# Four small changes of order, of awaited counts and of the engine of a copy in a one-core decoder step

## What is computed

```python
def hybrid_layer(x, k_past, v_past, C0, n0, m0, q_start, ...):
    xn = rmsnorm(x, ln1_w)
    z = xn @ w_in                       # 1024 -> 3592 columns
    ...                                 # qa, ka, va, qm, km, vm, om, gates are columns of z
    attn = moba_attention(qa, k_all, v_all, q_start)   # softmax over own and selected blocks
    h, C, n, m = mlstm_chunkwise(qm, km, vm, i_pre, f_pre, C0, n0, m0)
    h = ... * sigmoid(om)               # norm per head, output gate
    x = x + concat([attn, h]) @ w_out
    hn = rmsnorm(x, ln2_w)
    x = x + square(relu(hn @ w_up)) @ w_down
    return x, ka, va, C, n, m
```

## Time and profile before

| | us |
|---|---|
| median of 3 runs | 699.6 |
| lowest and highest | 699.0, 699.85 |
| profiled execution | 699.11 |
| its span | 697.4 |
| PE busy | 681.3 (98%) |
| DVE busy | 449.9 (65%) |
| ACT busy | 296.3 (42%) |
| POOL busy | 322.6 (46%) |

### The profile page before, as it was taken

How to read it: one execution, slowest core, us unless ns; L and a number is a source line. 1 busy time by engine, 2 the same in 40 slices (tenths; PEclk the granted TensorE clock), 3 DMA queues, 4 the chain that set the end, 5 groups by cost and what they waited for, 6 DMA issues and landing times.

```text
span 697.4 us, 15167 instructions
## 1 busy us (share of the span) xinstructions
PE 681.3 (98%) x5547; PEld 638.8 (92%) x5547; DVE 449.9 (65%) x894; ACT 296.3 (42%) x568; POOL 322.6 (46%) x232
## 2 busy tenths in 40 slices
PE   6999999999999999999999999999999999999996
PEld 6999988788687777999999999999999999999996
DVE  4598899986243456537798685867557576585134
ACT  6532735465342233245555443343433534334222
POOL 6739999823231544247337517062260623507431
PEclk9999999999999999999999999999999999999999
DMA  7946999944486788623111323332241331413103
GB/s 246 303 122 168 281 282 277 277 136 116 143 254 204 239 283 172 168 81 122 61 59 64 121 70 127 109 118 86 87 124 69 120 108 66 130 61 121 61 1 124
DMA packets 88633, 100.41 MB, mean 144 GB/s; under 512 B 5374, under 2 KB 64338, under 8 KB 88570
## 3 DMA queue, kind: packets, MB, share of 16 engines
q1 hardware_dynamic: 74566, 92.91, 42.9%
q10 hardware_dynamic: 14004, 6.67, 4.1%
HBM read 92.92 MB, written 6.64 MB: 143 GB/s over the span
## 4 chain that ended last, share of the span: by engine, by line
PE 80%; DVE 10%; issue 3%; POOL 3%; ACT 2%; DMA 1%; DVEq 0%; POOLq 0%; ACTq 0%
PE acc L914 7%; PE acc L915 6%; PE acc L916 6%; PE acc L1417 5%; PE acc L1418 5%; PE acc L1416 5%; PE scr L1417 3%; PE scr L1418 3%; PE scr L1416 3%; PE scr L1383 3%; PE scr L1382 3%; PE scr L1384 3%; PE acc L1382 3%; PE acc L1383 3%; PE acc L1384 3%
## 5 line engine op out<-in xcount | busy, mean ns | idle before, releaser
L914 PE MATMUL acc<-act_hi,w_hi 128*128 128x256 f32 (+1 forms) x416 | 120.8, 290 | 1.1 <-DVE zT L2503 1.1
L2017 POOL TENSOR_TENSOR h_lo<-relu,h_hi 128x520 fp32r<-128x520 f32 x32 | 44.0, 1379 | 164.8 <-ACT h_hi L1803 164.5
L915 PE MATMUL acc<-act_lo,w_hi 128*128 128x256 f32 (+1 forms) x416 | 117.3, 282 | 0.0
L916 PE MATMUL acc<-act_hi,w_lo 128*128 128x256 f32 (+1 forms) x416 | 117.2, 282 | 0.0
L1502 POOL TENSOR_TENSOR w_lo<-raw,w_hi 128x1024 fp32r<-128x1024 f32 x24 | 57.2, 2387 | 97.6 <-ACT w_hi L1495 95.2
L1970 POOL TENSOR_TENSOR prod<-kv,Qb 128x1024 f32<-128x1024 f32 x32 | 85.7, 2714 | 14.1 <-DVE S L2205 11.1
L914 PEld LDWEIGHTS acc<-act_hi,w_hi 128*128 128x128 f32 x416 | 78.4, 188 | 4.0 <-issue 2.3
L915 PEld LDWEIGHTS acc<-act_lo,w_hi 128*128 128x128 f32 x416 | 78.4, 189 | 0.5
L916 PEld LDWEIGHTS acc<-act_hi,w_lo 128*128 128x128 f32 x416 | 78.3, 188 | 0.0
L2522 DVE TENSOR_TENSOR xT<-acc,xT 128x260 f32<-128x260 f32 x64 | 26.7, 426 | 48.4 <-PE acc L1418 48.4
L2503 DVE TENSOR_TENSOR zT<-acc,rstd 128x264 f32<-128x264 f32 (+1 forms) x56 | 23.5, 421 | 43.1 <-PE acc L916 40.4
(11 more groups left out here) (418 smaller groups left out, 2298.4 us busy)
## 6 DMA issues: line engine op xcount, KB each, us to landing
kv<-in_cache_k_dram SPq DMA_DIRECT2D x64, 256.0 KB, 3.4
kv<-in_cache_v_dram SPq DMA_DIRECT2D x64, 256.0 KB, 3.1
raw<-in_w_up_dram SPq DMA_DIRECT2D x16, 1024.0 KB, 5.5
raw_d<-in_w_down_dram SPq DMA_DIRECT2D x12, 1024.0 KB, 5.1
raw<-in_w_in_dram SPq DMA_DIRECT2D x14, 512.0 KB, 6.0
raw<-in_w_in_dram SPq DMA_DIRECT2D x7, 1024.0 KB, 7.4
x_tok<-in_x_prompt_dram SPq DMA_DIRECT2D x8, 512.0 KB, 5.3
raw<-in_w_out_dram SPq DMA_DIRECT2D x4, 1024.0 KB, 7.3
```

The source lines that it names most:

```text
L914: pe.matmul(out, W_HI[home(g)][:, k, :], hi[k][:, cols], start=(n == 0), stop=False)
L915: pe.matmul(out, W_HI[home(g)][:, k, :], lo[k][:, cols], start=False, stop=False)
L916: mm = pe.matmul(out, W_LO[home(g)][:, k, :], hi[k][:, cols], start=False, stop=(n == KT - 1))
L2017: pool.tensor_tensor(h_lo[:, t, :], relu2[:, t % 2, :], h_hi[:, t, :].bitcast(F32), ALU.subtract).then_inc(s_hs_lo, 1)
```

## The change

Four edits:
1. In `banks()` the first three plain products of the MLP, in accumulator banks 0, 1 and 2, wait for 70, 71 and 72 copied half groups; before, all three waited for 72. Their order is the same.
2. In `plan()` rows_M goes from slot 6 to 7, rows_s and rows_end from slot 7 to 8.
3. Of att_t (1, 0) the second piece, 128x384, is copied by ACT and no longer by DVE.
4. sm_rt and sm_r are entered ahead of sm_c, so that in slots 50 to 52 they come first. The jobs are numbered anew with them.

```diff
--- before.py
+++ after.py
@@ -159,8 +159,9 @@
     at(3, ("gates", 1), ("rstd", 0))
     at(4, ("gates", 0), ("qs_tok",))
     at(5, ("qb", 0), ("qb", 1), ("rows_f",), ("rows_sum",))
-    at(6, ("rows_max",), ("rows_M",))
-    at(7, ("rows_s",), ("rows_end",))
+    at(6, ("rows_max",))
+    at(7, ("rows_M",))
+    at(8, ("rows_s",), ("rows_end",))
     at(12, ("gcols",))
     for t in range(4):
         at(11 + 2 * t, ("tokk", t))
@@ -214,11 +215,12 @@
     at(55, ("om_mix", 2), ("om_mix", 3))
     at(46, ("sm_prep",))
     at(48, ("vs_tok",))
+    for two in range(NS // 2):
+        at(51 + two, ("sm_rt", two))
+    for two in range(NS // 2):
+        at(50 + two, ("sm_r", two))
     for b in range(NS):
         at(49 + b // 2, ("sm_c", b))
-    for two in range(NS // 2):
-        at(50 + two, ("sm_r", two))
-        at(51 + two, ("sm_rt", two))
     at(54, ("sm_den",))
     at(55, ("sm_out",), ("pv_end",))
     at(56, ("sm_rs",), ("sm_end",))
@@ -356,7 +358,7 @@
 
 def banks():
 
-    use, last = {}, {b: ("out", N_HALVES) for b in range(3)}
+    use, last = {}, {b: ("out", N_HALVES - 2 + b) for b in range(3)}
     last.update({b: ("scr", b - 4) for b in range(4, 8)})
     for kind, e in PHASES:
         if kind == "plain":
@@ -1727,7 +1729,8 @@
                     elif e == 0:
                         act.wait_ge(s_out_m, 32)
                         evacuated(act, "gcols", 0)
-                    for n, col, end_col in ((0, 0, A_COL[1]), (2, A_COL[2], PW)):
+                    parts = (0, 0, A_COL[1]), (1, A_COL[1], A_COL[2]), (2, A_COL[2], PW)
+                    for n, col, end_col in parts if (t, e) == (1, 0) else parts[::2]:
                         copy_out(pTs[e][:, col:end_col], full(act, "att_t", t, e, n)[:, 0:end_col - col],
                                  "att_t", t, e, n)
                 elif name == "mix_att":
@@ -2448,8 +2451,9 @@
                     elif e == 0:
                         dve.wait_ge(s_out_m, 32)
                         evacuated(dve, "gcols", 0)
-                    free(dve.tensor_copy(pTs[e][:, A_COL[1]:A_COL[2]],
-                                         full(dve, "att_t", t, e, 1)[:, 0:A_COL[2] - A_COL[1]]), "att_t", t, e, 1)
+                    if (t, e) != (1, 0):
+                        free(dve.tensor_copy(pTs[e][:, A_COL[1]:A_COL[2]],
+                                             full(dve, "att_t", t, e, 1)[:, 0:A_COL[2] - A_COL[1]]), "att_t", t, e, 1)
                 elif name == "mix_att":
                     t, = a
                     dve.wait_ge(s_mix_hi, t + 1)
```

## The result

| | before | changed |
|---|---|---|
| median, us (22 runs each) | 699.0 | 700.18 |
| lowest, highest | 698.14, 700.32 | 699.77, 702.35 |
| profiled execution, its span | 699.11, 697.4 | 700.77, 699.0 |

The changed kernel takes 1.002 times as long, 95% interval 1.0014 to 1.0026: 1.2 us lost where 0.1 was forecast as gained. The profiled execution of the changed kernel is itself 0.6 above its median, so its rows show some 0.5 us more loss than the medians.

The account below looks back on a forecast made before the run. PE was taken to bound the kernel, with DVE and POOL a second stream absorbing its gains. Terms 0 + 0.05 + 0.04 + 0 = 0.09 us off 699.11 gave 699.0; against the 699.6 median, forecast 699.5, range 698.0 to 700.6.

Parts of the forecast that it names:

- The term: Slots 50 to 52: state transposes and small products going first gain PE 0.04 us; the half group starts at 261.86.
- The wait in slot 51: Near 261: about 0.4 us of PE's wait for DVE's state updates moves from the transposes to the small products.
- the cover fails: Slot 52: DVE's last updates, some 0.45 us later, are no longer hidden by its 1.69 us wait for PE: +0.45.
- Rival C: Before 149: DVE and POOL fall into another step, two w_lo stretch to 3.29 us, v_tok 2.0 later: 701.5 us; chance 0.06.
- S of 129.67: DVE reduction at 129.67 that waits for POOL's product; forecast to stay, a start elsewhere would mean a slower time.
- Edit 2: Near 49: removes PE's 0.87 us wait, lost again near 67, 87.23, 109 and 119; gain 0, bounds -0.87 and +0.4.
- Edit 3: At 125.91: removes PE's 1.42 us wait, lost again at 148.2 to 149.65; gain 0.05, bounds -1.42 and +0.49.
- The rule of the Trainium skill weighed for edit 3: Where DVE is saturated, giving work to ScalarE may make sense; by it the 1.42 us would be kept.
- its 0.5: First MLP product starts 0.5 us earlier, near 333.3; lost again near 371 at p_copy, gain taken as 0.
- D: Places of the removed waits: something else comes as late, so waits of 0.87 and 1.42 stay; 699.6 us, chance 0.03.
- A: All four places: the removed waits are real gains, 3.2 us together; 696.4 us, chance 0.06.
- B: At 149.65: only the gain of the ACT copy, 1.42 us, is kept as v_tok moves ahead; 698.1 us, chance 0.08.

Follow-up runs that it names:

- the same moves: Kernel before, without the four edits, with three plan steps moved (tokv 3; mx_t and own; mx_b) in slots 32 to 34: 698.94 us, ratio 0.9999.
- the moved plan: Changed kernel with POOL's w_lo waiting for m_h in slot 52, and tokv 3, mx_t, own and mx_b moved in slots 32 to 34: 697.16 us, ratio 0.9972.

## Why the prediction failed

**The step that failed: edit 4.** "Neither POOL nor any DMA moves" was read from the order, and the order on POOL is indeed the same. Its time is not. The term was -0.04, with bounds of -0.40 and +0.45; it measured +1.2 (700.28 against 699.05 for edit 4 alone). The wait in slot 51 went as forecast or better (0.19 where 0.4 was named); slot 52 did not. I followed the reordering along PE and DVE and stopped there; ACT's copy of sm_rows behind line 1092, w_hi behind that copy and POOL's w_lo behind w_hi were not followed. The bound of +0.45 took "the cover fails" to mean DVE's own reordering, not an instruction of four times its length. That 700.18 still lies between the forecast's 698.0 and 700.6 is luck: these were laid around a median of 699.6 from three executions; 22 give 699.0, and around that they would have ended at 700.0.

**Rival C had the mechanism and the wrong place.** It sought meetings of DVE and POOL at w_lo on DVE, up to 149, held that the phase is locked there, and gave 0.06 to a loss. There it held: DVE's longest w_lo in the profile after is 2.57 us (3.29 before). S of 129.67 did start elsewhere, which the forecast had named as a sign of C, but what moved it was the landing of keys. The meeting came at 263, where POOL makes w_lo itself and no reduction locks its phase to DVE's products. The page cited for C, the Trainium skill, "SBUF — State Buffer", section "Who interferes with whom", bears on it: a DVE instruction with two inputs in SBUF, as m_h is, contends with GpSimd's reads. The trace agrees, 0.68 us when 0.51 ahead of POOL's w_lo, 2.88 when 0.15 behind it. The page's section "SBUF: two separate sides" adds that for such an instruction too whichever starts first keeps the pair to its end. The trace agrees here as well: m_h, due 0.15 behind the start of w_lo, ends 0.55 behind its end, about its own length.

**Edit 2** was right: 1.0 off PE at 48.65, all of it back by 87.25. **Edit 3** was right in what it removes and where it goes back. That this happens at lines 1183 and 1137 and by those banks is shown by the run in which they are freed earlier: 1.8 us faster than the same moves without the edits. The rule of the Trainium skill weighed for edit 3 ("Perfetto Trace Analysis", section "Optimizing Scalar/DVE Operations") gave nothing that could be measured with edits 1 and 2 (1.0001); the time came with them (0.997) once the later meeting was out of the way.

**Edit 1.** The changed kernel's first MLP product waits for nothing. PE's lag behind the kernel before, 1.9 us at 270, shrinks to 1.11 there (334.95 against 333.84) and is back at 1.78 at the product behind p_copy (372.76 against 370.98):

```profile
347.91 0.82 PE L1292 MATMUL scr<-ident,rs 128*128 128x128 f32 x5 [0.22 <-POOL rs L1925]
...
372.76 0.39 PE L1384 MATMUL acc<-act_hi,w_hi 128*128 128x260 f32 x1
```

```profile
372.35 0.36 ACT L1818 ACTIVATE p_copy<-acc 128x260 f32<-128x260 f32 x1
```

About half goes back at 347 to 349 (the lag is 1.48 there), at and behind a wait for POOL that I had not named, the rest at p_copy. Only the trace shows this; no run was made to test it. With edits 1 to 3 worth nothing together, no part of its 0.5 was kept that the runs could measure. **D** fell with the waits gone. **A and B** fell; B's 1.42 is about what the moved plan brings back (1.8).

## What to carry to other kernels

An unchanged order on an engine says nothing of when its instructions start: after a reordering, follow each instruction to the engine that it releases, and from there to the next, until one is found that did not move. Where DVE products with two SBUF operands stand within half a microsecond of a long POOL instruction that reads SBUF, note which comes first: here that order was worth 2.2 us of DVE's time, nearly POOL's whole instruction. And a wait removed in front of a stream that is not slowed by it pays only when the next place where they meet is moved too.

## What was not expected of the hardware

The engines do not meet only at semaphores, as the first section has it: DVE and POOL met here in the middle of two instructions that wait for nothing of each other. Such a meeting leaves no idle time in the profile. It shows as one instruction of 2.88 us among its like of 0.68, and counts as busy time. The keys' landing varies: POOL waited 0.6 to 1.9 us for them, in one to three places, in the profiles of the nine kernels, all with the same order of loads.
